# The head of an expert loop: two banks for the first rows, and another order on VectorE

## The reference, cut to what matters

```
def ec_moe(h, w_router, w_gate, w_up, w_down):     # h: 1 x 1024 x 1024, 16 experts
    cap = EC_FACTOR * s // N_EXPERTS                # 128 tokens each
    aff = jax.nn.softmax(jnp.einsum('bsd,de->bse', h, w_router), axis=-1)
    gates, idx = lax.top_k(aff.transpose(0, 2, 1), cap)
    xs = jax.vmap(lambda hb, ib: hb[ib])(h, idx)
    g = jnp.einsum('becd,edf->becf', xs, w_gate)    # 1024 -> 512
    u = jnp.einsum('becd,edf->becf', xs, w_up)
    y = jnp.einsum('becf,efd->becd', jax.nn.silu(g) * u, w_down)   # 512 -> 1024
    y = y * gates[..., None].astype(y.dtype)
    return scatter-add of y to its tokens
```

## Time and profile before

| what | value |
| --- | --- |
| median of 3 runs | 3849.83 us (3845.61 to 3852.26) |
| the profiled execution | 3851.06 us, span 3849.3 us |
| PE busy | 3564.0 us (93%) |
| VectorE busy | 2520.6 us (65%) |
| ScalarE busy | 1853.2 us (48%) |
| GpSimd busy | 271.5 us (7%) |
| DMA | 607.63 MB, mean 158 GB/s |

### The profile page before, as it was taken

One profiled execution on the slowest core, in us unless ns is written; L12 is line 12 of the kernel. 1 busy time (PEld: TensorE's weight loads), 2 busy tenths in 40 slices (PEclk: granted clock), 3 DMA queues, 4 the chain that ended last, 5 costly groups with the idle time before them and its releaser, 6 DMA issues. The chain is left out here.

```text
span 3849.3 us, 57810 instructions
## 1 busy us (share of the span) xinstructions
PE 3564.0 (93%) x23078; PEld 2958.7 (77%) x23078; DVE 2520.6 (65%) x3931; ACT 1853.2 (48%) x2531; POOL 271.5 (7%) x178
## 2 busy tenths in 40 slices
PE   7999999989999999999999996799898999994996
PEld 4778888877777888887898775688786877774885
DVE  4477674488758677667333654788674766637886
ACT  4224432177334444434124753477535766533775
POOL 0000000100000000000000000244000000000542
PEclk9999999999999999999999998899998999997998
DMA  5011225531523337753323224699623031043997
GB/s 209 28 49 61 88 72 175 191 137 36 202 92 119 150 131 287 261 203 132 119 62 130 74 109 167 217 398 400 215 61 114 29 135 45 24 176 138 392 396 290
DMA packets 229433, 607.63 MB, mean 158 GB/s; under 512 B 30456, under 2 KB 130600, under 8 KB 211136
## 3 DMA queue, kind: packets, MB, share of 16 engines
q1 hardware_dynamic: 212896, 546.91, 38.1%
q0 software_dynamic: 13168, 55.16, 4.9%
q10 hardware_dynamic: 3120, 2.10, 0.2%
HBM read 483.38 MB, written 120.73 MB: 157 GB/s over the span
## 5 line engine op out<-in xcount | busy, mean ns | idle before, releaser
L4485 DVE TENSOR_TENSOR ring_r<-ring,oN_r 128x4096 fp32r<-128x4096 f32 x48 | 212.2, 4422 | 33.0 <-ACT oN_r L4390 33.0
L171 PE MATMUL scans_G<-ring_r 128*128 128x512 f32 x512 | 204.6, 400 | 0.0
L4259 POOL TENSOR_TENSOR moe_taker<-moe_zero 128x1 f32<-128x1 f32 x64 | 164.9, 2577 | 376.7 <-ACT moe_y L4471 346.8
L1433 DVE CUSTOM_DVE_ANT_0 oN<-heads_scores,heads_table 128x1024 f32<-128x1024 f32 x128 | 156.0, 1220 | 42.5 <-issue 42.5
L4390 ACT ACTIVATE oN_r<-ring 128x4096 fp32r<-128x4096 f32 x48 | 173.9, 3627 | 13.6 <-DMA ring<-in_w_all 12.3
L172 PE MATMUL scans_G<-hT_r,ring_r 128*128 128x512 f32 x448 | 175.1, 391 | 0.0
L173 PE MATMUL scans_G<-ring_r 128*128 128x512 f32 x448 | 175.0, 391 | 0.0
L1388 ACT ACTIVATE oN<-oN,heads_nm 128x1024 f32<-128x1024 f32 x128 | 146.7, 1146 | 23.4 <-DVE heads_nm L1433 20.2
L172 PE MATMUL mlp_ps<-mlp_room_r,ring_r 128*128 128x512 f32 x384 | 150.4, 392 | 0.0
L1351 PE MATMUL heads_turned<-identity,oN 128*128 128x128 f32 x1024 | 140.2, 280 | 2.7 <-ACT oN L1384 1.6
L1351 PEld LDWEIGHTS heads_turned<-identity,oN 128*128 128x128 f32 x1024 | 109.6, 140 | 37.5 <-issue 29.7
(11 more groups left out here) (811 smaller groups left out, 10811.3 us busy)
## 6 DMA issues: line engine op xcount, KB each, us to landing
ring<-in_w_all SPq DMA_DIRECT2D x78, 2048.0 KB, 15.2
moe_more<-in_w_all SPq DMA_DIRECT2D x16, 2048.0 KB, 15.6
hT<-in_w_all SPq DMA_DIRECT2D x16, 2048.0 KB, 16.3
hidden_operands<-mlp_room SPq DMA_DIRECT2D x56, 512.0 KB, 2.6
ring<-in_w_mlp SPq DMA_DIRECT2D x38, 512.0 KB, 5.7
ring<-in_w_mlp SPq DMA_DIRECT2D x8, 2048.0 KB, 8.1
ring<-in_w_all SPq DMA_DIRECT2D x12, 1024.0 KB, 6.2
branch_gates<-scans_stg SPq DMA_DIRECT2D x48, 256.0 KB, 2.0
```

What stands on the lines that cost most here:

```text
L171: pe.matmul(out, lh, rh, start=start, stop=False)
L1433: dve.tensor_tensor_reduce(out=sc[:, u % 3, :], in0=SA[:, 2 * (u % 2):2 * (u % 2) + 2, :].rearrange("p a n -> p (a n)"), in1=table[:], sca ...
L4259: pool.tensor_tensor(taker[:, n:n + 1], zero[:], zero[:], ALU.add)
L4485: dve.tensor_tensor(w_low[n % DEEP], w_raw[n % DEEP], w_high[n % HIGHS].bitcast(F32), ALU.subtract)\
```

## The change

It does three things, all in `moe_stage`. The first expert's two halves are turned into two different banks, TP and AP, without a wait in between (`turn_first`, `take_first`, `low_first`). The wait of a gate product for its rows is parted: ahead of k = 0 it waits for half 0, ahead of k = 4 for half 1, in the head and in the loop. On VectorE `low(0, 3)` moves behind `gated(0, 0)` and the last `low_x` of the head. GpSimd's gathers stay as they are.

```
+            def turn_first(half):
+
+                bank = (TP, AP_)[half]
+                for k in range(4):
+                    kk = 4 * half + k
+                    ins = pe.transpose(bank[:, k, :], xs[:, 0, kk * P:(kk + 1) * P], ids[:])
+                ins.then_inc(xt_done, 1)
...
                 pe.wait_ge(w_split, i * SLOTS + n + 1)
                 if what is G:
-                    pe.wait_ge(xt_in, i * (2 * EJ) + 2 * (j + 1) + 1)
                     pe.wait_ge(gu_free, i * EJ + (j + 1))
                 w = w_views(n, KD)
                 for k in range(KD):
+                    if what is G and k % 4 == 0:
+                        pe.wait_ge(xt_in, i * (2 * EJ) + 2 * j + k // 4 + 2)
                     ins = three_passes(pe, what[:, j % 2, :], [x_[:, j % 2, k, :] for x_ in (x_high, x_low)],
                                        [w_[:, k, :] for w_ in w], k == 0, k == KD - 1)
                 ins.then_inc(done, 1)
 
+            pe.wait_ge(xs_in[0], 16)
             for half in range(2):
-                turn_x(0, 0, half)
+                turn_first(half)
...
+            def take_first(half):
+                act.wait_ge(xt_done, half + 1)
+                act.activation(x_high[:, 0, 4 * half:4 * half + 4, :], (TP, AP_)[half][:, :, :], ACT.Copy).then_inc(xt_cast, 1)
...
             for half in range(2):
-                take_x(0, 0, half)
+                take_first(half)
...
+            def low_first(half):
+                of = slice(4 * half, 4 * half + 4)
+                dve.wait_ge(xt_cast, half + 1)
+                dve.tensor_tensor(x_low[:, 0, of, :], (TP, AP_)[half][:, :, :], x_high[:, 0, of, :].bitcast(F32), ALU.subtract)\
+                   .then_inc(xt_in, 1)
...
             for half in range(2):
-                low_x(0, 0, half)
+                low_first(half)
             low(0, 1)
             low(0, 2)
             low_x(0, 1, 0)
-            low(0, 3)
             gated(0, 0)
             low_x(0, 1, 1)
+            low(0, 3)
```

## The result

The change takes 3828.84 us (median of 5, 3824.53 to 3831.12) against 3849.69 us (5 runs) before: ratio 0.9947, 95% interval 0.9935 to 0.9958, 20.9 us less. The forecast was 3829.3 us. The profiled execution has a span of 3829.4 us, 19.9 us less than before.

The account below looks back on a forecast made before the run. The prediction took the experts' stage to be bound by PE, with the DMA engines as full. Four head terms, 10.5 us in layer 0 and 10.05 in layer 1, together 20.5 us, took 3849.8 us to 3829.3 us, range 3825 to 3832.

Parts of the forecast that it names:

- Two banks and parted waits: Head of each layer: G(0) starts after the first x_low instead of both, 2.07 us earlier a layer.
- The clock in G(0): First gate product: runs at full clock because PE idles less before it, gaining 1.61 us in layer 0, 1.54 in layer 1.
- The rival in which it still falls: G(0) stays at the lower clock; 1.61 and 1.54 us stay spent, 3832.5 us with both; chance 0.13.
- The wait of 4.33 us: PE's idle time ahead of G(1) goes entirely with VectorE's new order: 4.33 us in layer 0, 4.32 in layer 1.
- The slow G(1): With no idle time ahead, G(1) runs at full clock, gaining 2.47 us in layer 0 and 2.12 in layer 1.
- low(0, 3) last: VectorE in the head: low(0, 3), now last, ends 1.7 us before U(1) needs it; new order costed at nothing.
- The wait inside G: Added semaphore wait between matmuls 12 and 13 of 32 gate products: taken as 0, other end 2.9 us in all.
- the sign of being wrong: Inside G: a start between matmuls 12 and 13 over 0.3 us after the one before would show the forecast wrong.
- The transfers: Weight loads in the stage: earlier issue overlaps loads and costs 0 to 0.7 us a layer; 0 taken.
- The cover of 0.14 us at the 13th expert: Late in the stage: a_low ends 0.14 us before PE needs it, so backlog added relative to PE would reduce the gain.
- The rival named the right resource: In the experts' stage, transfers take back some or nearly all of the gain, up to 3842.5 us; chance 0.09.
- The sum: Both layers' heads: 10.5 us in layer 0 and 10.05 us in layer 1, together 20.5 us less.

Follow-up runs that it names:

- undivided wait: The change with each gate product again waiting for both halves at its start; two banks and VectorE's order kept: 3829.30 us, ratio 0.9947 to the kernel before.
- the order alone: The kernel before with only low(0, 3) moved behind gated and the head's last x_low on VectorE: 3833.62 us against 3848.51, ratio 0.9957.
- busy-work in the wait: The kernel before with 24 instead of 6 pairs of busy-work matmuls behind expert 1's transposes: 3844.80 us against 3851.50, ratio 0.9985.
- all but the order: The change with low(0, 3) put back ahead of gated; two banks and parted wait kept: 3830.63 us, ratio 0.9952 to the kernel before.
- the gathers ahead of the scatters: The change with each further gather issued ahead of the scatter instead of behind it: 3857.98 us, ratio 1.0016 to the kernel before.
- more transfers: The change with 128 KB more transferred behind each weight load, to an unread scratch tensor: 3851.65 us against 3851.50, ratio 1.0000 to the kernel before.

## Why the prediction was right

- **Two banks and parted waits, 2.07 us a layer.** Measured 2.01 and 2.02 us (4.15 to 2.14). The size is right, the cause named only half right: with one bank and a parted wait 1.7 of them come too (first transposes to G(0) 2.45 us), with two banks and an undivided wait 1.5 (2.68 us).
- **The clock in G(0), 1.61 and 1.54 us.** Measured 1.61 and 1.54 us. That the clock would hold was a choice between two values, at 0.13 for the other, and no row read then could decide it; that it came out is in part luck. Its reason was loose too: the "quarter" of idle time counts G(0)'s own first matmuls as busy; from the first transposes to G(0) PE is idle 1.07 of 2.14 us, before 2.88 of 4.15. The rival in which it still falls didn't occur, neither here (granted clock 1.00) nor in the nine other kernels whose G(0) starts early (5.5 to 5.6 us each). In every kernel that keeps both idle times (before, the order alone, busy-work in the wait) G(0) takes 6.9 to 7.2 us.
- **The wait of 4.33 us.** Gone in both layers. The prediction gave it to VectorE's order "entirely"; shown is that the order alone does it but for 0.4 us, and that without the order the parted wait leaves 1.5 us of it.
- **The slow G(1), 2.47 and 2.12 us.** Measured 2.48 and 2.14 us, and by the busy-work in the wait shown to come from PE's idleness: filling it takes all of the slowness away.
- **low(0, 3) last, at nothing.** 1.75 us of cover in the profile, 1.7 by the prediction.
- **The wait inside G, at nothing.** The starts around it are at most 0.23 us apart in all 32 gate products, and the sign of being wrong was 0.3 us.
- **The transfers.** 0 to 0.7 us were allowed a layer and 0 taken. The landings keep to 20 us, no wait for weights of over 0.15 us came. The cover of 0.14 us at the 13th expert, from which I had argued, was misread in two ways. a_low is the low part of `gated`'s result, and is late because it stands behind a weight's low part on VectorE. And 0.10 us is what stands between a_low's end and Y's start where PE does wait, so only 0.04 us were left. The change used that up at the 14th expert of layer 0, for 0.14 us. The longer waits, with the change and where the busy-work is left out, are for gathered rows, which the prediction took to keep their place to PE, and the kernel before has such waits too. The rival named the right resource and the wrong queue in front of it. That the transfers can bind, as its price said, the run with more of them shows: 11.7 us a layer. The Trainium skill, DMA: Bandwidth & Descriptors, in "Where 436 GB/s comes from", has about 358 GB/s for the memory side, and beside it a measured transfer at 425 GB/s. Taken as a bound of this one core the 358 disagrees with the trace, after the change as before it: 397 GB/s in the middle of the stage.
- **The sum.** 10.48 and 10.05 us by the prediction, 10.68 and 10.27 us measured in the heads. The 0.2 us are G(1)'s start: the idle time of a row is counted from the modelled end of the busy-work, which is later than the moment at which the next matmul could have started. In all 20.5 us forecast and 20.9 us measured by medians. So close a match of the whole is partly luck: the interval of the ratio reaches from 16 to 25 us, and 0.8 us of the gain came in the rests, where none was forecast. What bears the forecast out is the heads. The profiled executions differ by 1 us less than that, because the time between the stages, untouched by the change, happened to be 3.3 us longer.

The rule of the Trainium skill, TensorE: Matmul & The Clock Gate, in "Part 1: The HAM clock gate", not to fit the number of slow matmuls since it varies from run to run, is given there for the matmuls at a kernel's start. Applied here it would have given 12.8 us. In this kernel's heads the rows were the better guide: over the three kernels that keep both idle times, the slow G(0)s lie within 0.3 us of each other.

## What to carry to other kernels

Price an idle time of PE with the slow matmuls behind it: here 4.3 us of waiting cost 2.1 to 2.5 us more, and 2.9 us in two pieces 1.6 us more, and both came back with the wait. Where a product needs its operand in parts, waiting part by part is worth as much as making the operand earlier, and makes the order on the other engines matter less. Before moving a transfer forward in a queue, look at what it then stands behind: changing which transfer is issued at the old place brought the rows earlier for nothing, moving the place cost 25 us, 8 of them by the clock.

## What the hardware showed that I had not expected

Idle times of 1.07 us (the change), 1.62 us (undivided wait) and 1.51 us in the middle of G(1) (all but the order) left the granted clock at 1.00, while two of 1.4 us, with transposes of 0.6 us between them, brought it to 0.50 each time. The length of an idle time alone doesn't tell: with the gathers ahead of the scatters it fell after all five waits of 2.7 to 3.5 us and not after those of 2.4 and 1.6 us, without the busy-work it held after one of 2.1 us, and with more transfers it fell after one of 1.87 us. A stage whose 16 DMA engines are reported full at 397 GB/s, with landing times growing from 8 to 20 us (layer 0), ran with some 0.2 us of PE's waits behind late low parts; asked for a further 128 KB with every 2 MB it lost 4% of its time (11.7 of 289 us).
